# One quad of weight pieces per pair of column blocks in Strassen's form, in both MLPs

## The reference, cut to what matters

```
def sq_relu_mlp(h, w_up, w_down):           # h 256 x 2048, w_up 2048 x 8192, w_down 8192 x 2048
    return jnp.square(jax.nn.relu(h @ w_up)) @ w_down
...
h = h + sq_relu_mlp(rms_norm(h, mlp_norm_w[l]), w_up[l], w_down[l])
```

## Time and profile before

| | us |
|---|---|
| median of 3 runs | 2457.65 |
| lowest and highest run | 2457.37, 2458.85 |
| span of the profiled execution, first to last instruction | 2456.4 |
| TensorE busy in it | 2441.9 |
| VectorE busy | 1539.9 |
| ScalarE busy | 1195.5 |
| GpSimd busy | 259.1 |

### The profile page before, as it was taken

The page is one execution under the profiler, slowest core; times in us unless marked ns, Lnnn a source line. Parts: engine busy times, 40 slices in busy tenths (PEclk is TensorE's granted clock), DMA queues, the critical chain, the costliest instruction groups (busy, mean ns, idle before and its releaser), DMA issues.

```text
span 2456.4 us, 32498 instructions
## 1 busy us (share of the span) xinstructions
PE 2441.9 (99%) x11683; PEld 2039.3 (83%) x11683; DVE 1539.9 (63%) x1664; ACT 1195.5 (49%) x1442; POOL 259.1 (11%) x394
## 2 busy tenths in 40 slices
PE   8999999999999999999999999999999999999999
PEld 7888888888888888888888888888888888888887
DVE  5788888875565555565555766666655565565554
ACT  5556555654444344344444545555544444444443
POOL 1011111111011000010011111110110010010010
PEclk9999999999999999999999999999999999999999
DMA  7777777777678677677687766655886686786785
GB/s 205 225 225 228 230 223 228 224 222 238 216 230 241 193 228 230 191 233 223 193 245 238 235 202 194 187 176 175 262 244 213 204 237 207 210 240 197 219 237 169
DMA packets 288103, 535.30 MB, mean 218 GB/s; under 512 B 22318, under 2 KB 55440, under 8 KB 286976
## 3 DMA queue, kind: packets, MB, share of 16 engines
q1 hardware_dynamic: 264736, 457.87, 61.3%
q0 software_dynamic: 22976, 75.91, 11.2%
q10 hardware_dynamic: 288, 0.11, 0.0%
HBM read 498.09 MB, written 35.72 MB: 217 GB/s over the span
## 4 chain that ended last, share of the span: by engine, by line
PE 99%; DMA 1%; DVE 0%; ACT 0%; SPq 0%; issue 0%; ACTq 0%
PE acc L422 18%; PE acc L424 18%; PE acc L423 18%; PE aux L424 12%; PE aux L423 12%; PE aux L422 12%; PE aux L438 1%; PE aux L439 1%; PE aux L437 1%; PE aux L510 1%; PE aux L452 1%; DMA resid<-in_x 1%; PE acc L504 0%; PE aux L653 0%; PE aux L654 0%; PE aux L560 0%
## 5 line engine op out<-in xcount | busy, mean ns | idle before, releaser
L1095 DVE TENSOR_TENSOR w_lo<-w_raw,w_hi 128x1024 fp32r<-128x1024 f32 x865 | 1053.5, 1222 | 824.6 <-ACT w_hi L741 824.0
L741 ACT ACTIVATE w_hi<-w_raw 128x1024 fp32r<-128x1024 f32 x865 | 913.2, 1060 | 1076.9 <-PE acc L424 545.6
L422 PE MATMUL acc<-w_hi,stationary 128*128 128x512 f32 x1984 | 778.5, 392 | 0.0
L424 PE MATMUL acc<-w_hi,stationary 128*128 128x512 f32 x1984 | 773.2, 390 | 0.0
L423 PE MATMUL acc<-w_lo,stationary 128*128 128x512 f32 x1984 | 773.0, 390 | 0.0
L422 PE MATMUL aux<-w_hi,stationary 128*128 128x512 f32 x1340 | 522.1, 390 | 0.0
L424 PE MATMUL aux<-w_hi,stationary 128*128 128x512 f32 x1340 | 521.9, 389 | 0.0
L423 PE MATMUL aux<-w_lo,stationary 128*128 128x512 f32 x1340 | 521.8, 389 | 0.0
L424 PEld LDWEIGHTS acc<-w_hi,stationary 128*128 128x128 f32 x1984 | 372.5, 188 | 77.9
L422 PEld LDWEIGHTS acc<-w_hi,stationary 128*128 128x128 f32 x1984 | 372.6, 188 | 76.4
L423 PEld LDWEIGHTS acc<-w_lo,stationary 128*128 128x128 f32 x1984 | 372.7, 188 | 75.9
(11 more groups left out here) (206 smaller groups left out, 1170.3 us busy)
## 6 DMA issues: line engine op xcount, KB each, us to landing
w_raw<-in_w_up SPq DMA_DIRECT2D x256, 512.0 KB
w_raw<-in_w_down SPq DMA_DIRECT2D x256, 512.0 KB
w_raw<-in_ssm_w_in SPq DMA_DIRECT2D x129, 512.0 KB
w_raw<-in_ssm_w_out SPq DMA_DIRECT2D x64, 512.0 KB
w_raw<-in_w_kv SPq DMA_DIRECT2D x64, 512.0 KB
spread<-work POOLq DMA_DIRECT2D x44, 512.0 KB, 3.8
work<-spread POOLq DMA_DIRECT2D x176, 128.0 KB, 5.0
w_raw<-in_ssm_w_in SPq DMA_DIRECT2D x64, 256.0 KB
```

What stands on the lines that cost most here:

```text
L422: pe.matmul(o, xh, hi[:, k], start=start, stop=False)
L424: mm = pe.matmul(o, xl, hi[:, k], start=False, stop=stop)
L741: a.activation(whi[:, s, :], raw[:, s, :], ACT.Copy).then_inc(sem("hi_made"), 1)
L1095: v.tensor_tensor(wlo[:, s, :], raw[:, s, :], whi[:, s, :].bitcast(F32), ALU.subtract).then_inc(sem("lo_made"), 1)
```

## The change

**Pairs and quads.** The column blocks are taken in pairs (halves 0 and 1). A chunk has four pairs: p = 0 and 1 of the up product, p = 2 and 3 of the down product. In every pair of an MLP but the very first, four pieces (4 k-tiles by 2 column blocks, the *quad*: k-tiles 12 to 15 of the up product, 0 to 3 of the down product) are treated as a 2 x 2 block matrix, with the activations of these k-tiles as another (two k-pairs by the two halves of the tokens). Their product takes seven block products instead of eight, in Winograd's order of Strassen's form:

```diff
+            def form_piece(unit, form, region, start):
+                pe.wait_ge(sem("lo_made"), unit + 1)
...
+                for k in range(2):
+                    xh, xl = (form_tile(form, region, k, i) for i in range(2))
+                    pe.matmul(o, xh, hi[:, k], start=start and k == 0, stop=False)
+                    pe.matmul(o, xh, lo[:, k], start=False, stop=False)
+                    mm = pe.matmul(o, xl, hi[:, k], start=False, stop=alone and k == 1)
+                mm.then_inc(sem("w_used"), 1)
...
+                def relu(c, u):
+                    a.wait_ge(sem("half_read"), 2 * U + 8 * c + u + 1)
+                    a.activation(sums[u % 2], sums[u % 2], ACT.Relu).then_inc(sem("relu_made"), 1)
+                    a.wait_ge(sem("relu_made"), U + 4 * c + u + 1)
+                    a.activation(sums[u % 2], sums[u % 2], ACT.Square).then_inc(sem("up_made"), 1)
...
+                def t1_t3(made):
+                    v.wait_ge(sem("quad_in1"), 32 * (made + 1))
+                    v.tensor_tensor(quad[:, 0, :], quad[:, 1, :], quad[:, 0, :], ALU.subtract).then_inc(sem("t_made"), 1)
+                    v.wait_ge(sem("quad_in3"), 32 * (made + 1))
+                    v.tensor_tensor(quad[:, 1, :], quad[:, 3, :], quad[:, 1, :], ALU.subtract).then_inc(sem("t_made"), 1)
...
+                def add_forms(unit, made):
+                    v.wait_ge(sem("form_copied"), made + 1)
+                    v.wait_ge(sem("w_used"), unit + 6 + 1)
+                    p1, u2, u3, c22 = sums[0][:, 0, :], sums[1][:, 0, :], sums[0][:, 1, :], sums[1][:, 1, :]
+                    link(v.tensor_tensor(u2, form_bank["P6"], p1, ALU.add))
+                    link(v.tensor_tensor(u3, form_bank["P7"], u2, ALU.add))
+                    v.tensor_tensor(u2, form_bank["P5"], u2, ALU.add)
+                    v.tensor_tensor(c22, form_bank["P5"], u3, ALU.add).then_inc(sem("forms_read"), 1)
+                    v.wait_ge(sem("forms_read"), made + 1)
...
+            def add_half(layer, n, unit):
+                half = n % 2
+                v.wait_ge(sem("w_used"), unit + 1)
+                v.tensor_tensor(sums[half], halves[half][:, :, :], sums[half], ALU.add).then_inc(sem("half_read"), 1)
...
+                            if j == 0:
+                                t1_t3(made)
...
+                            if p == 1:
...
+                                if not late and j == 3:
+                                    add_half(layer, 1, start - 1)
+                                if not late and j == 5:
+                                    turn_up(c, 1)
+                                if j == (8 if late else 5):
+                                    up_sums(c)
+                                    up_lo(c, 0)
+                                if j == (11 if late else 8):
+                                    sums_lo(4, 2 + c, sums[0])
+                                if j == 11:
+                                    up_lo(c, 1)
...
+                            if j == (13 if late else 10):
+                                add_forms(start, made)
```

More of the change, by code:

```diff
@@ new lines, in mlp @@
+                n = 0
+                for c in range(4):
+                    for p, (at, units) in enumerate(chunk_pairs(c)):
+                        done = 0
+                        following = (c, p + 1) if p < 3 else (c + 1, 0)
+                        for what, half, kt in units:
+                            if what != "d":
+                                continue
+                            direct_load(n, weights(c, p, half, kt))
+                            n, done = n + 1, done + 1
+                            left = len([u for u in units if u[0] == "d"]) - done
+                            if following[0] < 4:
+                                for i in {5: (1,), 3: (0,), 2: (3,), 1: (2,)}.get(left, ()):
+                                    quad_load(i, *following, base + chunk_start(c) + at)
@@ L1558, in _ @@
                 last = h[:, t, 3 * NB:]
[L1559 removed]
+                v.scalar_tensor_tensor(last, halves[1][:, t, :], h_rs[:, t:t + 1], last, ALU.mult, ALU.add).then_inc(sem("last_added"), 1)
         @block.gpsimd
```

489 lines of the change are left out of this document (359 added, 130 removed).

## The result

The changed kernel is slower. Its median of 4 runs is 2497.55 us (2496.77 to 2500.51), beside 2457.51 us for 4 runs of the kernel before on the same chip: a ratio of 1.0164 with an interval of 1.0149 to 1.0178. I had forecast 2442.5 with a range of 2424 to 2466. The profiled execution is the slowest of the four, 3.0 us above the median. The removed matmuls are gone; TensorE waits for more than they were worth.

The account below looks back on a forecast made before the run. TensorE, busy 99%, was taken as the bound: matmul count times spacing. 40.8 us saved less stalls of 18.5, 6.2 and 1.0 left 15.1 gained, so 2442.5 us from a span of 2456.4 (median 1.25 longer); range 2424 to 2466.

Parts of the forecast that it names:

- The saving: TensorE, thirty formed pairs: 180 fewer matmuls at 0.2267 us each save 40.8 us if TensorE never waits.
- p = 1: Second up-product pair, chunks 1 to 3: VectorE's bursts stall TensorE 3.1 us a pair, six times, 18.5 us.
- the wait on an own result: VectorE's sums of products: three of four are followed by a 0.13 us wait; 3.1 us for all four sums.
- The last pair of the first MLP: Residual turns and products on VectorE stall TensorE at units 4, 9, 11 and 12, 6.2 us in all.
- p = 2: First down-product pair: margins 0.25 to 0.9 us; last turned quarter takes 11 us, at 14 about 1 us stall.
- full use: Second half of a pair: nine loads in about 15 us, issued early enough to cost 0, bounds 0 to 3.
- The walk: Unit-by-unit layout of VectorE's and ScalarE's queues with traced durations, giving each pair's margins and stalls of TensorE.
- The clock: Rival: seven stalling pairs each drop the clock once, 2.3 us apiece, 16 us on top, 2458.5 us; chance 0.03.
- The rival on the slower side: VectorE bounds the first part of every formed pair; at 0.1 us more per operation, 2476 us; chance 0.13.
- a wrong main step: Signs: waits in p = 2 and 3 as in p = 1, ending on DMA, moved spacing or clock, or under 10 us.
- The forecast case: Whole kernel: TensorE stalls of 15 to 36 us take back part of what is saved, 2433 to 2452.7 us; chance 0.53.
- "hidden": Rival: VectorE's and ScalarE's queues overlap better, stalls only 5 to 15 us, 2417 to 2432 us; chance 0.15.

Follow-up runs that it names:

- experiment 6: Kernel before, with 6 of 12 matmuls of one weight piece left out in each of thirty pairs (180 in all), nothing added: 2417.91 us, ratio 0.9838.
- experiment 3: Changed kernel, with p = 1's token sums, sums of products and quarter reads moved to the later units that chunk 0 uses: 2486.77 us, ratio 1.0126 to the kernel before.
- Experiments 2: Changed kernel, with quad loads bringing only 16 of 512 columns, except in the first formed pair of each MLP: 2444.87 us, ratio 0.9946 to the kernel before.
- experiment 8: Changed kernel, with quad loads issued behind the 9th, 10th and 11th direct load of a pair, not the 7th, 9th, 10th and 11th: 2456.06 us, ratio 0.9996.
- experiment 1: Changed kernel, with the last turned quarter in p = 2 read behind unit 14 instead of 12 on ScalarE and VectorE: 2447.68 us, ratio 0.9963 to the kernel before.
- experiment 5: Kernel before, with chains of idle adds on VectorE at ten places of the MLPs to make TensorE wait on purpose: 2499.33 us in one run.

## Why the prediction was wrong

**The saving: right within 4%.** 40.8 us forecast, 39.4 to 39.6 measured in experiment 6.

**p = 1: right, a little high.** I had 3.1 us a pair, at units 6, 9 and 11 (1.0, 0.3, 1.8), and 18.5 in all. The trace has 0.63 and 1.27 of wait at units 6 and 11, 2.7 us a pair with the restarts, 16.4 in all; experiment 3 got 10.8 to 14.8 back. What was too high: the wait on an own result, which I had put at 0.13. The four sums of products start at 923.40, 924.12, 924.84 and 925.45 with 0.68 or 0.69 each, so 0.04 and 0.03 us lie between the first three, which depend on one another; from first to last they take 2.7 us where I had 3.1. The token sums take 1.4 from the end of the turn (912.34 to 913.77) and not 1.6. VectorE's pitch was the one forecast.

**The last pair of the first MLP: right in its sum** (6.2 forecast, 6.0 measured), and at the units named, where 2.1, 1.3, 1.2 and 1.6 turned out as 1.9, 0.8, 0.8 and 1.9. But I stopped there. The attention's first pieces behind it waited another 3.2 and dropped the clock, 5.3 us in all that no term had.

**p = 2: the step that failed.** I wrote that the last turned quarter takes "11 us in all, 14 with the longest of 8.4", and a stall of about 1 us at 14. The p = 2 pairs had a term of less than 1.0 us and cost 52. In the trace it takes 15.4 us from turn to read in one pair and 17.2 to 18.7 in the other seven. Both pieces of the working were off: 3.97 to the second set of DMAs was 6.2 at 957.66, and from there to the read, 1.75 and 5.0 or at most 8.4, it was 10.6 (963.84 to 974.44). I took these durations from a trace in which no quad load existed, and in the same text wrote that nine loads in 15 us were "full use". That sentence asked only whether the loads would come in time for themselves. What else was on the DMA engines at that moment, the very transfer that unit 13 hangs on, I didn't ask. The bound was wrong too: it has a stall of 1.5 us in "all six p = 2 pairs", and there are eight. Experiments 2 and 8 show the cause by taking away the bytes and the moment, and experiment 1 shows that even so the length alone did no harm; it is the length with the read at unit 12.

**The walk was right and its reach too short.** I looked for the margin at unit 13 by the queue of VectorE, where it was some 0.7 us. With a read that comes 3 us later than the longest that I had allowed, every one of these microseconds stalls both engines, since no hi can pass the read on ScalarE. A margin below 1 us on a term whose bounds are 11 and 14 should have been priced over more than those bounds.

**The clock: a price near the right one, at the wrong places.** I had 2.3 us a drop, worked out from the kernel's start, and gave it 0.03, behind the seven pairs that I had stalling. It is 1.7 in most cases and up to 2.8. But not one of these seven dropped the clock, with gaps up to 1.78 us. It fell behind the p = 2 gaps and at the attention's first pieces, which the forecast didn't have. The Trainium skill (TensorE: Matmul & The Clock Gate, "HAM oscillation — how this bites in real kernels") holds that waits for data between groups of matmuls send TensorE back to 1.2 GHz. The trace agrees at every p = 2 gap of the kernel after (2.52 to 5.43 us) and behind six of the ten gaps of experiment 5, and doesn't behind the other four. The one row that I had against it, the gap of 0.27 us in the earlier trace rows, was about ten to twenty times shorter than the gaps in question. A gap of 2 us or more should be priced with its drop.

**The rivals.** That a wait for a transfer would take the place of TensorE's work wasn't among them; I had it only as a sign at the end, for the loads, and not for the quarters. The rival on the slower side named VectorE, with 0.05 to 0.06 us more per operation as its point of decision; VectorE's operations weren't slower at all (a lo takes 1221 ns in the mean, 1222 before). The lists of waits name VectorE's lo (L1616) for 44.9 of some 55 us, and whoever stops at that name confirms the wrong rival: the row for ScalarE, 77.7 us for `work<-spread`, is the one that tells. Two of the signs that the prediction named for a wrong main step are there: the waits stand in p = 2 more than in p = 1, and their chain ends on a DMA.

**A sum.** The forecast case (stalls of 15 to 36 us) comes to 2431.9 to 2452.9 by its own terms, where the prediction has 2433 to 2452.7, and "hidden" (5 to 15) to 2421.9 to 2431.9, where it has 2417 to 2432. Nothing hangs on either.

## What to carry to other kernels

Where data come back through DRAM, place the engine's read of them as late as its consumer allows, since everything behind the read on that engine waits too; here moving it by two units was worth 50 us of 2498, with the same operations in all. Time such a trip in the load pattern of the new kernel, not the old one, and give a wait on TensorE of over 2 us its price with the clock, here 1.7 us more in most cases. Fewer matmuls (39.5 us) pay only once nothing new waits: the form as first ordered lost 1.6%, and with its reads and sums put later it gains 1.2%.

## What the runs showed of the hardware that I had not expected

- **A drop of the clock has a price, but the length of the gap doesn't decide whether it comes.** 1.5 to 1.7 us in most cases, 1.9 to 2.8 us where the stretch at 1.2 GHz is twice as long and begins in the gap, after gaps of 1.77 to 5.62 us; gaps of 1.77, 2.27 and 3.62 us left the clock at 1.00 in other places. The 40 digits on the profile's page showed none of it.
- **Loads on the hardware queue stretch a transfer of POOL's queue far beyond their own time.** One quad load of 512 KB more, issued 1.0 us ahead of the quarter's trip, went with a read at 17.0 us instead of 10.9 (1134.81 in the kernel after, 1120.51 in experiment 8), where the load by itself is worth 1.72 us by the forecast's price. Queue 1's share over the span says nothing of it: it fell from 61.3% to 58.1%. Why it is 6 us and not 2 is open; no run tests it. The rows suggest one way: in experiment 8 POOL's second step (1124.55 to 1126.88) is out before the next quad load (1127.47), and in the kernel after that load (1141.76) falls inside the step (1140.58 to 1142.90).
- **VectorE's wait for its own result was 0.03 to 0.04 us** between sums of 512 elements out of PSUM, where the one row before the change had shown 0.13.
- **Spread.** Experiment 8 ran between 2449.84 and 2461.74 in its 10 runs, 0.5% wide, beside 0.1 to 0.3% for the others, of 4, 5 or 15 runs.
